# Two transformer blocks on one core: the delta heads taken into buffers that come free under the last two input projections

## What is computed

```python
h = rmsnorm(x, norm_w)
proj = h @ w_in                       # 4 x 512 (attention) + 4 x 512 (delta: q, k, v, z) + 4 x 4 gate columns
attn = neighbourhood_attention(rmsnorm(aq), rmsnorm(ak), av, rpb) * silu(az)    # 8 heads of 64, four pairs
dq, dk, dv = split(silu(conv5(cat(dq, dk, dv))))                                # depthwise, 5 taps
# 4 delta heads of 128, forward and backward in time, chunks of 64 tokens:
#   (u, w) = inverse(I + strict_lower(kb k^T * decay)) @ (v beta, kb exp(g))
#   v_new = u - w S;  o = (q exp(g)) S + intra v_new;  S = S exp(g_last) + k'^T v_new
delta = rmsnorm(o_forward + o_backward) * silu(dz)
x = x + cat(attn, delta) @ w_out
```

## Time and profile before

| what | value |
|---|---|
| runs of the kernel before | 2315.35, 2324.99, 2326.78 us, median 2324.99 |
| the profiled execution | 2318.85 us |
| its span, first to last instruction | 2317.1 us |
| PE, busy in the span | 2192.8 us (95%) |
| DVE, ACT, POOL | 1092.1, 947.4, 389.3 us |
| mean granted PE clock | 0.97 of full |

### The profile page before, as it was taken

How to read it: one execution, slowest core, us unless ns; L and a number is a source line. 1 busy time by engine, 2 the same in 40 slices (tenths; PEclk the granted TensorE clock), 3 DMA queues, 4 the chain that set the end, 5 groups by cost and what they waited for, 6 DMA issues and landing times.

```text
span 2317.1 us, 29035 instructions
## 1 busy us (share of the span) xinstructions
PE 2192.8 (95%) x11559; PEld 1793.0 (77%) x11559; DVE 1092.1 (47%) x2025; ACT 947.4 (41%) x1713; POOL 389.3 (17%) x594
## 2 busy tenths in 40 slices
PE   7886899999788799999999999999999999999998
PEld 5775767767688688887887788787888888888886
DVE  5665444433147434566545665555614342433441
ACT  4644354444345233555455554553313232232220
POOL 5011617403302210000000000003301211010111
PEclk9888999999889899999999999999999999999999
DMA  4355553412562422112111211112121111344232
GB/s 143 109 168 178 163 133 84 101 56 52 178 238 90 142 91 79 37 37 73 35 48 33 68 60 46 37 46 69 48 80 46 46 55 48 126 134 162 92 104 86
DMA packets 169672, 209.76 MB, mean 91 GB/s; under 512 B 36320, under 2 KB 122816, under 8 KB 168000
## 3 DMA queue, kind: packets, MB, share of 16 engines
q1 hardware_dynamic: 148848, 140.71, 19.6%
q0 software_dynamic: 20688, 67.19, 9.2%
HBM read 150.41 MB, written 53.77 MB: 88 GB/s over the span
## 4 chain that ended last, share of the span: by engine, by line
PE 86%; DVE 4%; ACT 3%; DMA 3%; issue 2%; POOL 1%; SPq 1%; DVEq 0%; POOLq 0%; ACTq 0%
PE PS L1735 13%; PE PS L1737 12%; PE PS L1736 12%; PE PS L1729 9%; PE PS L1731 9%; PE PS L1730 9%; PE PS L1695 5%; PE PS L2020 3%; PE PS L1999 3%; PE PS L1829 2%; PE PS L1806 2%; DMA RAW<-in_w_in 1%; DVE WH L2449 1%; PE PS L2052 1%; PE PS L2065 1%
## 5 line engine op out<-in xcount | busy, mean ns | idle before, releaser
L1735 PE MATMUL PS<-WH,HH 128*128 128x512 f32 x1344 | 549.1, 409 | 3.9 <-DVE WK L2504 3.9
L1737 PE MATMUL PS<-WH,HL 128*128 128x512 f32 x1344 | 528.4, 393 | 0.0
L1736 PE MATMUL PS<-WH,HH 128*128 128x512 f32 x1344 | 527.5, 392 | 0.0
L1729 PE MATMUL PS<-HH,WH 128*128 128x512 f32 (+1 forms) x976 | 403.2, 413 | 24.2 <-DVE WH L2449 24.2
L1731 PE MATMUL PS<-HH,WH 128*128 128x512 f32 (+1 forms) x976 | 385.4, 395 | 0.0
L1730 PE MATMUL PS<-HL,WH 128*128 128x512 f32 (+1 forms) x976 | 385.1, 395 | 0.0
L1735 PEld LDWEIGHTS PS<-WH,HH 128*128 128x128 f32 x1344 | 255.1, 190 | 61.5 <-issue 10.5
L1737 PEld LDWEIGHTS PS<-WH,HL 128*128 128x128 f32 x1344 | 254.1, 189 | 55.5
L1736 PEld LDWEIGHTS PS<-WH,HH 128*128 128x128 f32 x1344 | 255.4, 190 | 45.5
L2449 DVE SCALAR_TENSOR_TENSOR WH<-RAW,WK,WH 128x512 fp32r<-128x512 f32 (+2 forms) x248 | 185.2, 769 | 209.0 <-ACT WH L2074 208.4
L1729 PEld LDWEIGHTS PS<-HH,WH 128*128 128x128 f32 (+1 forms) x976 | 184.8, 189 | 64.5 <-DVE WH L2449 26.8
(11 more groups left out here) (317 smaller groups left out, 2907.5 us busy)
## 6 DMA issues: line engine op xcount, KB each, us to landing
RAW<-in_w_in SPq DMA_DIRECT2D x200, 256.0 KB, 3.0
RAW<-in_w_out SPq DMA_DIRECT2D x32, 256.0 KB, 3.4
sig_d<-WK POOLq DMA_DIRECT2D x32, 256.0 KB, 2.4
WK<-sig_d POOLq DMA_DIRECT2D x32, 256.0 KB, 3.2
WK<-in_rpb POOLq DMA_DIRECT2D x16, 480.0 KB, 3.8
RAW<-in_w_in SPq DMA_DIRECT2D x32, 192.0 KB, 3.3
dnc_d<-TM SPq DMA_DIRECT2D x12, 512.0 KB, 4.8
TM<-dnc_d SPq DMA_DIRECT2D x10, 512.0 KB, 4.2
```

What stands on the lines that cost most here:

```text
L1729: e.matmul(ps, wh, hh, start=k == 0, stop=False)
L1735: e.matmul(ps, hh, wt[:, 0:width], start=k == 0, stop=False)
L1736: e.matmul(ps, hh, wt[:, 512:512 + width], start=False, stop=False)
L1737: mm = e.matmul(ps, hl, wt[:, 0:width], start=False, stop=k == 7)
```

## The change

- `DA`, `DV`, `DT`, `LT`, `XB`, `parts` and `ZT` give each head other buffers. Head 2 lies in `TM[:, 0]`, `TM[:, 2]`, `EXT` and the slot of the norms; head 0 in the first token half of the input operand; head 1 in the second; head 3 in `TM[:, 1]` and in the area of attention.
- The input operand `HHa`/`HLa` becomes two halves by tokens, `[128, 2, 8, 512]`, so the first half is free after `dz`'s fourth tile.
- `EXT`, 12 KB per partition, is new; the scratch for DMA descriptors shrinks from the default 16384 bytes to 4096. The gate `dz` goes to `WHF` (first half) and `EXT` (second half), which is free when head 2's `e2` has ended.
- `share(h)` issues each head's loads on its own conditions; the streams of the heads are spawned before `gemm` of `dz`, in the order 2, 0, 3, 1. The loads `lt` and `lx` are items of their own.
- Head 1's recursion uses banks 0 and 1 after `dz`; each finished head gives its banks back to the ring.
- `wo0` starts its first tile before the turned heads are there: only products with k >= 4 wait, each for the head in the order 2, 0, 3, 1 (`MIXED`, which also orders the rows of `w_out`).
- `dn` and `na0` evacuations wait in streams (`leave`, `leave_first`) instead of draining the plan. Many costs of `work` and times in the streams of `conv` and `solve` are changed. The residual `x` is read once heads 2 and 3 are through.

```diff
-        "dl": [("bus", 7500), ("dma", 2000)],
-        "dv": [("bus", 4000), ("dma", 2000)],
+        "dl": [("bus", 4800), ("dma", 2000)],
+        "dv": [("bus", 3100), ("dma", 2000)],
+        "lt": [("bus", 3100), ("dma", 2000)],
+        "lx": [("bus", 2200), ("dma", 2000)],
...
-        "cn": [("pe", 900), ("dve", 150)],
+        "cn": [("pe", 1750), ("dve", 150)],
...
+    def leave(b, t):
+
+        c, th = t
+        h = int(BLOCKS[b][2])
+        yield has("xb", 1)
+        yield has("g", b, t, 7)
+        if c < 3 and 3 * h + c >= NCONV:
+            before = divmod(3 * h + c - NCONV, 3)
+            yield has("cn", *before) if before[1] < 2 else has("cv", *before, 4)
+        put("ev", b, t)
+        if c < 3 and th:
+            plan.spawn(conv(h, c))
+
+    def leave_first(b, t):
+        yield has("cn", 3, 1)
+        yield has("cv", 3, 2, 4)
+        yield has("g", b, t, 7)
+        put("ev", b, t)
...
         put("cs", h, c)
         yield
+        plan.now[0] += 2500.0
+        yield
         plan.aside("cw", h, c)
         if c < 2:
             put("cq", h, c)
+            plan.now[0] += 6000.0
             yield
...
+    def share(h):
+
+        if h == 2:
+            yield has("nw", 2)
+            yield has("nx", 2)
+            yield has("da", 1)
+            for kind in ("dl", "lt", "dv", "lx", "dt"):
+                plan.aside(kind, h)
+                yield
+        elif h == 0:
+            yield has("g", X_LAST, 3, 7)
+            for kind in ("dl", "dv", "dt"):
+                plan.aside(kind, h)
+                yield
+            yield has("zs", 0)
+            plan.aside("lx", h)
+            yield has("no", 3, 0, 7)
+            yield has("no", 3, 1, 7)
+            put("lt", h)
+        elif h == 3:
+            yield has("nw", 3)
+            yield has("nx", 3)
+            yield has("w", 71)
+            for kind in ("lt", "dv", "lx", "dl", "dt"):
+                plan.aside(kind, h)
+                yield
+        else:
+            yield has("g", X_LAST, 7, 7)
+            yield has("dt", 3)
+            plan.both(*((kind, h) for kind in ("dl", "dv", "lt", "lx", "dt")))
...
+    def recursion(h):
+        yield has("e3", h, 1)
+        yield has("d2", h, "k", 1)
+        yield has("dt", h)
+        for x in range(2):
+            yield has("no", 3, x, 7)
+        if h == 1:
+            for x in (2, 0, 3):
+                yield has("e3", x, 1)
+                yield has("d2", x, "k", 1)
+            yield has("ev", X_LAST, 7)
+            use_ring([b for b in state["ring"] if b > 1], "rec1")
...
         if name == "dz":
-            plan.drain(has("da", 1))
             plan.spawn(gate_side())
+            for h in (2, 0, 3, 1):
+                plan.spawn(share(h))
+                plan.spawn(pre(h), 1)
+                plan.spawn(levels(h), 1)
+                plan.spawn(recursion(h))
+                plan.spawn(gate(h))
+                plan.spawn(finish(h))
+            plan.spawn(mix_load(), 3)
+            plan.spawn(mix_turn(), 3)
+            plan.spawn(mix_in(), 3)
+            plan.spawn(residual(), 3)
...
-        if name == "na0":
-            plan.drain(has("cn", 3, 1))
-            plan.drain(has("cv", 3, 2, 4))
...
+    plan.drain(has("st", "mix", 7, 0))
+    plan.drain(has("w", 79))
+    plan.drain(has("r2", 1, 7))
+    plan.drain(has("xr"))
+    use_ring(list(range(8)))
+
+    def merged_in(t, k):
+        if k >= 4:
+            plan.drain(has("st", "mxd", MIXED[k - 4], t // 4))
+
+    gemm(BLOCK["wo0"], None, None, merged_in)
...
-        HHa = lent.enter_context(nc.sbuf_tensor("HH", [128, 8, 1024], F32R))
-        HLa = lent.enter_context(nc.sbuf_tensor("HL", [128, 8, 1024], F32R))
+        HHa = lent.enter_context(nc.sbuf_tensor("HH", [128, 2, 8, 512], F32R))
+        HLa = lent.enter_context(nc.sbuf_tensor("HL", [128, 2, 8, 512], F32R))
...
+                        if t >= 4:
+                            w.wait_ge(*at["e2", 2, 1, "q"])
...
-    nc = bacc.Bacc("TRN2", target_bir_lowering=False, num_devices=1)
+    nc = bacc.Bacc("TRN2", target_bir_lowering=False, num_devices=1, dynamic_dma_scratch_size=4096)
```

More of the change, by code:

```diff
@@ L422, in waiting @@
     def waiting(held):
-        return held and held[:2] == ("tile", 0) and ("g", *held[1:], 7) in plan.known and ("ev", *held[1:]) not in plan.known
+        return held and held[0] == "tile" and held[1] < 5 and ("g", *held[1:], 7) in plan.known and ("ev", *held[1:]) not in plan.known
     def take(item):
@@ new lines, in give_back, with gate, finish @@
+    def give_back(h):
+        plan.known["rec", h] = plan.known["r2", h, 7]
+        state["ring"] = state["ring"] + [BANK_A[h], BANK_B[h]]
+        for b in (BANK_A[h], BANK_B[h]):
+            holder[b] = ("rec", h)
+    def gate(h):
+        for x in range(2):
+            yield has("no", 3, x, 7)
+        yield has("zs", 1)
+        yield has("e3", 0 if h in (0, 2) else 3, 1)
+        put("fz", h)
+    def finish(h):
+        yield has("r2", h, 7)
+        give_back(h)
+        put("f1", h)
+        yield has("fz", h)
+        put("f2", h)
+        yield has("r2", 1, 7)
+        st("mxd", h)
+        if h == 1:
+            limit[0] = 8 * len(BLOCKS)
@@ L736, in schedule, with mix_load, residual @@
+    def mix_load():
+        yield has("zs", 1)
+        yield has("nw", 3)
+        yield has("dt", 1)
+        yield has("r2", 2, 7)
+        plan.both(*(("ld", "mix", n) for n in range(3)))
+        for t in range(5):
+            yield has("st", "mix", t, 0)
+            put("ld", "mix", t + 3)
+    def residual():
+        yield has("f1", 2)
+        yield has("f1", 3)
+        put("xr")
     plan.spawn(solve())
@@ L758, in schedule @@
             if n == 0:
+                for t in range(8):
+                    plan.drain(has("ev", b, t))
                 use_ring([0, 1], "na")
@@ L855, in mix_load @@
-    def mix_load():
-        plan.both(*(("ld", "mix", n) for n in range(3)))
-        for t in range(5):
-            yield has("st", "mix", t, 0)
-            put("ld", "mix", t + 3)
-    plan.spawn(share())
-    for h in range(4):
-        plan.spawn(pre(h), 1 + h // 2)
-        plan.spawn(levels(h), 1 + h // 2)
-        plan.spawn(recursion(h))
-        plan.spawn(gate(h))
-        plan.spawn(finish(h))
-    plan.spawn(mix_turn(), 3)
-    plan.spawn(mix_in(), 3)
-    plan.drain(has("nw", 3))
```

382 lines of the change are left out of this document (199 added, 183 removed).

## The result

| | before | after |
|---|---|---|
| median | 2322.25 us (11 runs, 2315.35 to 2329.07) | 2334.63 us (11 runs, 2326.71 to 2345.95) |
| profiled execution | 2318.85 us | 2343.62 us |
| span | 2317.1 us | 2341.8 us |

The ratio after to before is 1.0056, 95% interval 1.0035 to 1.0077: the changed kernel is slower, by some 12 us. The prediction said 2263 us and faster. The profiled execution of after is itself 9.0 us above its median, so of the 24.8 us between the two profiled executions about 12 belong to the change.

What follows compares the result with a forecast made beforehand. TensorE bounds the kernel, busy 2192.8 of 2317.1 us. Delta stage and way into wo0 46 us plus na0 16 us make 62 us off 2318.85: 2257 us profiled, 2263 us median, range 2238 to 2297 us.

Steps and rivals of the forecast that it cites:

- Part 3: na0's first product no longer waits behind head 3's second convolution, closing PE's 16.37 us stall: 16 us, bounds 0 to 22.
- the weight tile: na0's eighth weight tile would be late next once the stall is gone, costing 2 us.
- Part 1: Delta heads staggered, their loads and inversions earlier: stage done at 722 us; with Part 2, 46 us gained.
- dz's end at 628 us: Pushed by 8 us of inversion and other heads' products; head 1's loads follow, its recursion starts from 653 us.
- the inversion under the attention at 8 us: Head 2's inversion under na3's attention costs its own 8 us and takes them out of the later stage.
- 7.2 us a step: Head 1's recursion step with two or three heads beside it, against 6.8 us alone; through at 711 us.
- The ceiling of 62 us: Delta stage, dz's end to wo0: 167 us less 105 us of PE work, reached only if PE never waits.
- the "about 100" of the prediction: Sign of being right: dz's last to wo0's first product takes about 100 us instead of 167.
- Part 2: Way into wo0: 21 products of its first tile, 4.7 us, run ahead of the last head's result.
- Rival D: Slower: last head serial, dz's tiles queued behind the evacuation awaiting head 2's second level; 2345 us, chance 0.04.
- D's rule: wo0's effective start is head 1's first step + 57.6 + 12.5 - 4.7; both gains gone from 730 us.
- Rival C: Head 2's loads hold up na3's gathers on POOL and its attention; lone last head remains; 2294 us, chance 0.07.

Runs made afterwards that it cites:

- experiment 1: Kernel before with only the early part (dn and na0 evacuations in own streams, new conv and solve costs), heads unstaggered: 2290.56 us, ratio 0.9871.
- experiment 10: Kernel of experiment 1 measured again, beside another run on the same chip: 2292.87 us, ratio 0.9883.
- experiment 4: Changed kernel with the inversions of heads 0 and 3 and every head's recursion planned behind dz's last product: 2315.12 us, ratio 0.9971.
- experiment 5: Kernel of experiment 4 with head 2's transposes and inversion also moved behind the last attention: 2302.30 us, ratio 0.9917.
- experiment 6: Changed kernel with only head 2's transposes and inversion moved behind the last attention: 2344.19 us, ratio 1.0094.
- experiment 7: Kernel of experiment 5, but the inversions of heads 0 and 3 may stand ahead of dz's end: 2325.86 us, ratio 1.0020.
- experiment 8: Changed kernel with only the heads' loads staggered, all head arithmetic behind dz's last product: 2294.86 us, ratio 0.9883.
- experiment 11: Kernel of experiment 5 with head 1's loads held back until head 2's last step: 2310.22 us, ratio 0.9951.
- experiment 3: Kernel before with the descriptor scratch of 4 KB alone: 2320.80 us, ratio 0.9996.

## Why the prediction was wrong, point by point

**Part 3 (na0), right, and undersized.** 16 us forecast; dz begins 21.6 us earlier, and the early part alone gives 31 and 27 us in the medians of experiments 1 and 10. The bound of 22 us was too low. Late next was the weight tile, as worked out, with 3.2 us.

**Part 1, the step that failed: dz's end at 628 us.** It is 698.9 us, although dz began 21.6 us earlier than before. The sum took dz's end as 612 us, plus 8 for an inversion, plus the heads' products by their PE time. That leaves 8 us for the other heads ahead of dz's end. In after 42 us of their PE time stand between dz's last four tiles, by the prediction's own prices: the inversions of heads 0 and 3 and 232 of the 592 recursion instructions. To these come 12 us in which PE waits for copies between two items of a chain, and some 12 us of low clock. The prediction had read that a lone step takes 6.8 us of which PE works 2.2, and meant to fill those 4.6 us with dz's products as if PE could choose; but the planner had laid down which items go into each gap, and in a fixed order an item that waits holds up the dz product behind it. The sum had no term for the low clock. Experiments 4 to 7 show that the order does it: dz ends at 657 us with two inversions ahead of its end (42 us for 16 us of PE's work), at 615 us with none, at 695 us with the recursions too.

**Part 1, the inversion under the attention at 8 us.** Experiment 5 against 4 gives 7 to 13 us for its place, and dz's end at 615 us (5) against 588 us (8) shows what early loads and inversion together cost ahead of dz: 26 us. From dz's begin to its end 5 takes 105.3 us and 8 takes 77.7; of the 27.6 us between them 9.7 are idle time (10.2 against 0.5 us) and some 14 the low clock (0.84 against 0.96). PE's idle time while the loads fill the DMA engines, and the low clock that followed it, are what the rows of that stretch show beside the inversion's own time; the sum had no term for them.

**Part 1, 7.2 us a step.** Sound for heads side by side (6.7 us for three in experiment 11, 8.9 us for four in experiment 5), but that case never comes about in after: 13.4 us for head 2, 10 for heads 3 and 0.

**The ceiling of 62 us was no estimate.** The stretch between dz and wo0 did shrink to 96 us, the "about 100" of the prediction, but as the remainder of a longer whole. Even with dz's end kept (experiment 8) nothing of the delta part's 62 us was to be had, because behind the heads stand the last head's gate work and the attention's loads.

**Part 2.** The 10.0 us behind the last square were no longer all behind wo0: in after wo0's first product comes 7 us behind the last head's last subtraction, and the first product that needs this head 16.6 us behind it. What it is worth wasn't measured alone.

**Rival D came about, with 0.04.** Head 1's first step, PE in order of time in after:

```profile
739.51 1.06 PE L2094 MATMUL PS<-H 128*128 128x128 f32 x4
```

By D's rule (this start + 57.6 + 12.5 - 4.7) wo0 starts in effect at 804.9 us, 25.5 us behind the 779.4 us of before, and that makes 2344 us of the profiled 2318.85 us; the profiled execution of after took 2343.62 us. (The rule's 730 us at which both gains are gone is on the clock of before; the trace of after already holds the early lead.) That it fits to 1 us is partly luck: the first product that needs head 1 stands at 804.95 us, where the rule has 809.6 us, and the low clock and later stretches made up for it. But its mechanism was another: the prediction looked for dz's tiles behind the evacuation that waits for head 2's second level. The last products of that level start at 562.7 us, 46 us before dz's fifth tile begins (609.0 us, right behind the fourth), so that wait cost nothing; the tiles that follow were late by the inversions and steps between their own products. The prediction argued against D with head 2's early data, which has no bearing on what is queued ahead of dz.

**Rival C** in its POOL form did not happen (9.04 us for na3's gathers in after, 9.03 before), nor did the scratch matter (experiment 3). The loads beside the attention do fill the DMA engines, and that part of it is in the 26 us.

**Open.** What makes up the part of the 37 us that is neither idle time nor low clock; how the 26 us divide between loads and inversion, and how much of the 96 us tail in after, against 83 in experiment 11, is the attention's fourth load that stood behind eleven weight loads (26.96 us on SP, 737.88 to 764.88 us), and how much head 0's last steps.

## What to carry to other kernels

Work moved ahead of a stage on an in-order queue costs that stage its busy time and its waits, and here the low clock that went with them: two inversions of 16 us put dz's end off by 42 us. The busy time would have been spent anyway; the waits and the low clock are the loss. Before giving idle gaps to a chain, ask what has to end at the end of the stage (here dz, which held the buffers of the next loads), and let nothing with a wait stand ahead of it. Chains that wait on other engines were cheapest side by side: in this kernel, staggering them in time took away the very work that filled their gaps. And when a change has two parts, test each alone: here one part was worth 30 us and the other cost 40.

## What the runs showed of the hardware

Descriptor scratch of 4 KB instead of 16 KB made no difference to GpSimd's bursts of 16 DMA issues (9.06 us against 9.03 us). A stop of 4.33 us followed by 32-wide products was followed by a granted clock of 0.50 for more than 20 us of stretches in which PE was over 80% busy, where experiment 1's rows of the same stretches have 1.00, 0.83 and 1.00:

```profile
520.00:530.00 10.00, 4.33 (x82) 3.66 (x82) 1.73 (x3) 7.81 (x14) 0.00 (x0) 0.86 0.93 292
530.00:540.00 10.00, 8.26 (x117) 6.06 (x117) 2.58 (x11) 2.80 (x9) 0.58 (x1) 0.50 0.16 52
540.00:550.00 10.00, 9.32 (x50) 7.41 (x50) 1.20 (x4) 3.02 (x6) 0.00 (x0) 0.50 0.00 0
550.00:560.00 10.00, 9.22 (x50) 7.57 (x51) 2.67 (x8) 1.66 (x5) 0.00 (x0) 0.50 0.01 2
560.00:570.00 10.00, 10.00 (x40) 6.45 (x39) 2.44 (x11) 2.96 (x8) 0.00 (x0) 0.76 0.00 1
```

PE is 4.33 us busy in the first of these rows; the clock is half in the next three and comes back in the fifth. The three rows at half clock are 30 us, which cost about 15 us of work (an estimate), more than the 5.7 us that PE idles in the first row. The stop and the narrow products aren't the only thing that differs: with the same loads and no inversion there (experiment 5) the clock was still 0.60 and 0.71 in 520 to 540 us.
